# The first group's gates: transfers of combined weights and of split pieces issued by ScalarE instead of SyncE

## The reference, cut to what matters

```python
def mixer_a(h, w_in, ln_g, ln_b, w_s, b_s, w_out):
    u, v, z = jnp.split(h @ w_in, 3, axis=-1)
    u = jax.nn.gelu(u)
    v = layer_norm(jax.nn.gelu(v), ln_g, ln_b)
    ...
    mixed = jnp.einsum("gts,bnsgc->bntgc", ws, vc) + b_s.T[:, :, None]
    y = u * mixed.reshape(B, S, A_WIDTH) * jax.nn.silu(z)
    return y @ w_out
```

## Time and profile before

| what | value |
|---|---|
| median of three runs | 2218.93 us (2217.34 to 2219.06) |
| the profiled execution | 2219.44 us, its span 2217.7 us |
| PE | 2150.9 us busy, 97% |
| DVE, ACT, POOL | 1440.5 (65%), 1095.3 (49%), 1195.1 us (54%) |
| granted clock of PE, mean | 0.996 |
| SP's queue | 585.71 MB, 73.5% of the transfer engines' time |
| ACT's queue | 5.30 MB, 0.7% |

### The profile page before, as it was taken

The page is one execution under the profiler, slowest core; times in us unless marked ns, Lnnn a source line. Parts: engine busy times, 40 slices in busy tenths (PEclk is TensorE's granted clock), DMA queues, the critical chain, the costliest instruction groups (busy, mean ns, idle before and its releaser), DMA issues.

```text
span 2217.7 us, 29383 instructions
## 1 busy us (share of the span) xinstructions
PE 2150.9 (97%) x10410; PEld 1801.0 (81%) x10410; DVE 1440.5 (65%) x1761; ACT 1095.3 (49%) x2050; POOL 1195.1 (54%) x913
## 2 busy tenths in 40 slices
PE   5999999999999999999999999999999999999998
PEld 4887778788888878888777888887888888888887
DVE  6956548757486864554974673767767657656854
ACT  4334446634545744445653445534545646545653
POOL 3456675845553865544594645441535555454542
PEclk9999999999999999999999999999999999999999
DMA  9888889785558785557877556899686697887654
GB/s 347 307 306 308 312 315 356 231 308 174 196 198 324 285 315 191 200 179 269 314 259 283 181 181 218 323 348 365 244 297 225 253 359 266 280 309 288 206 205 171
DMA packets 244787, 592.89 MB, mean 267 GB/s; under 512 B 20929, under 2 KB 96801, under 8 KB 244257
## 3 DMA queue, kind: packets, MB, share of 16 engines
q1 hardware_dynamic: 241680, 585.71, 73.5%
q10 hardware_dynamic: 2960, 5.30, 0.7%
HBM read 461.96 MB, written 119.54 MB: 262 GB/s over the span
## 4 chain that ended last, share of the span: by engine, by line
PE 75%; DMA 6%; POOL 6%; DVE 5%; ACT 3%; DVEq 2%; POOLq 1%; issue 1%; SPq 1%; ACTq 0%
PE ps L2361 22%; PE ps L2363 22%; PE ps L2362 22%; DMA w_raw<-in_a_w_in 3%; POOL w_lo L1130 3%; PE ps L2566 2%; PE ps L2615 1%; PE ps L2616 1%; POOL cbl L1149 1%; PE ps L2641 1%; DVE acc L1812 1%; ACT w_hi L1364 1%; DMA w_lo<-a_weights_combined 1%; PE ps L2650 1%; DVE yb L2093 1%
## 5 line engine op out<-in xcount | busy, mean ns | idle before, releaser
L1130 POOL TENSOR_TENSOR w_lo<-w_raw,w_hi 128x1024 fp32r<-128x1024 f32 x244 | 650.0, 2682 | 569.6 <-ACT w_hi L1364 569.4
L1364 ACT ACTIVATE w_hi<-w_raw 128x1024 fp32r<-128x1024 f32 x260 | 272.0, 1057 | 418.3 <-DMA w_raw<-in_a_w_in 372.7
L2361 PE MATMUL ps<-h,w_hi 128*128 128x512 f32 x1024 | 403.3, 394 | 9.7 <-POOL w_lo L1130 8.3
L2363 PE MATMUL ps<-h,w_lo 128*128 128x512 f32 x1024 | 398.9, 390 | 0.0
L2362 PE MATMUL ps<-h,w_hi 128*128 128x512 f32 x1024 | 398.7, 389 | 0.0
L2361 PEld LDWEIGHTS ps<-h,w_hi 128*128 128x128 f32 x1024 | 192.2, 188 | 55.3 <-POOL w_lo L1130 14.3
L2363 PEld LDWEIGHTS ps<-h,w_lo 128*128 128x128 f32 x1024 | 192.2, 188 | 40.7
L2362 PEld LDWEIGHTS ps<-h,w_hi 128*128 128x128 f32 x1024 | 192.4, 188 | 38.9 <-issue 0.2
L2361 PE MATMUL ps<-r,w_hi 128*128 128x512 f32 x480 | 191.6, 399 | 1.9 <-issue 1.9
L2363 PE MATMUL ps<-r,w_lo 128*128 128x512 f32 x480 | 187.7, 391 | 0.0
L2362 PE MATMUL ps<-r,w_hi 128*128 128x512 f32 x480 | 187.3, 390 | 0.0
(11 more groups left out here) (277 smaller groups left out, 4902.6 us busy)
## 6 DMA issues: line engine op xcount, KB each, us to landing
w_raw<-in_a_w_in SPq DMA_DIRECT2D x256, 256.0 KB, 3.6
w_hi<-b_weights_split SPq DMA_DIRECT2D x104, 512.0 KB, 4.7
w_lo<-b_weights_split SPq DMA_DIRECT2D x104, 512.0 KB, 6.3
w_raw<-in_a_w_in SPq DMA_DIRECT2D x52, 512.0 KB, 4.7
w_raw<-in_a_w_out SPq DMA_DIRECT2D x48, 512.0 KB, 5.4
w_hi<-v_weights_combined SPq DMA_DIRECT2D x48, 512.0 KB, 3.9
w_lo<-v_weights_combined SPq DMA_DIRECT2D x48, 512.0 KB, 5.2
w_hi<-a_weights_combined SPq DMA_DIRECT2D x32, 512.0 KB, 6.6
```

Source lines behind the costliest of these rows:

```text
L1130: g.tensor_tensor(wlo[p][:, rows_], raw[p][:, rows_], whi[p][:, rows_].bitcast(F32), ALU.subtract).then_inc(w_lo, 1)
L1364: s_.activation(whi[p][:, rows_], raw[p][:, rows_], ACT.Copy).then_inc(w_hi, 1)
L2361: t_.matmul(dst_, stat[0], mov[0], start=start, stop=False)
L2363: return t_.matmul(dst_, stat[1], mov[0], start=False, stop=stop)
```

## The change

`load_split`, `keep_split`, `load_comb` and `keep_comb` move out of SP's block and get the issuing engine as an argument; their bodies stay as they are. In group 0 SP keeps only the combinations of stages up to 4 for loading (`q <= FIRST_BY_ACT + 1`) and those of stages below 3 for storing (`q - 2 < FIRST_BY_ACT`), and no split pieces. ACT takes the others: the loads of stage 4 + `g` ahead of `hi` of the next first unit (steps 1 to 7), the stores of stage 3 + `g` behind it, ahead of the gelus (steps 0 to 7). In groups 1 to 3 SP goes on as before.

```diff
+FIRST_BY_ACT = 3
...
+        def keep_comb(eng, c):
+            _, _, whose, n, m = COMBS[c]
+            eng.wait_ge(comb_lo, c + 1)
...
-            def keep_comb(c):
-                _, _, whose, n, m = COMBS[c]
-                sp.wait_ge(comb_lo, c + 1)
...
                 s = split_at(i, q - 2)
-                if s is not None:
-                    keep_split(s)
-                for c in combs_at(i, q - 2):
-                    keep_comb(c)
+                if s is not None and i >= 1:
+                    keep_split(sp, s)
+                if q - 2 < FIRST_BY_ACT:
+                    for c in combs_at(i, q - 2):
+                        keep_comb(sp, c)
                 if 1 <= q < GROUPS + 4:
                     unit(first + 2 * q + 1)
...
-                for c in combs_at(i, q):
-                    load_comb(c)
+                if q <= FIRST_BY_ACT + 1:
+                    for c in combs_at(i, q):
+                        load_comb(sp, c)
                 s = split_at(i, q)
-                if s is not None:
-                    if i == 0:
-                        sp.wait_ge(ada_used, 6 * KT)
-                    load_split(s)
+                if s is not None and i >= 1:
+                    load_split(sp, s)
...
                     if g == 0:
                         comb(i, 3)
                         split(i, 3)
+                    if i == 0 and g >= 1:
+                        for c in combs_at(0, 4 + g):
+                            load_comb(act, c)
+                        if split_at(0, 4 + g) is not None:
+                            act.wait_ge(ada_used, 6 * KT)
+                            load_split(act, split_at(0, 4 + g))
                     hi(uz_unit(i, g + 1, 0))
+                    if i == 0:
+                        for c in combs_at(0, 3 + g):
+                            keep_comb(act, c)
+                        if split_at(0, 3 + g) is not None:
+                            keep_split(act, split_at(0, 3 + g))
                     if g == GROUPS - 1:
                         factor_round(0, 0)
                         factor_round(1, 0)
```

More of the change, by code:

```diff
@@ L774, in landed, with load_split @@
             return 16 * sum(transfers(w) for w in range(u + 1) if BUFFER[w] == BUFFER[u])
+        wa = a_w_in[0].rearrange("(k p) n -> p k n", p=P)
+        wo2 = a_w_out[0].rearrange("(k e p) n -> p k e n", e=2, p=P)
+        wkv = w_kv.rearrange("(k p) n -> p k n", p=P)
+        wb = b_w_in[0].rearrange("(k p) n -> p k n", p=P)
+        wbo = b_w_out[0].rearrange("(k p) n -> p k n", p=P)
+        def load_split(eng, s):
+            m, (kind, n, ku), hh = SPLIT_SLOT[s], SPLIT_UNITS[s // 2], s % 2
+            kt = 4 * ku + 2 * hh
+            if split_before(s):
+                eng.wait_ge(split_out[m], 32 * split_before(s))
+            if kind == "kv":
+                there, src = wsr[m][:].rearrange("p a (b n) -> p (a b) n", b=2), wkv[:, 4 * hh:4 * hh + 4, :]
+            elif kind == "b":
+                there, src = wsr[m][:], wbo[:, kt:kt + 2, 512 * n:512 * n + 512]
+            else:
+                there, src = wsr[m][:, :, 0:256], wb[:, kt:kt + 2, 256 * n:256 * n + 256]
+                eng.dma_start(wsr[m][:, :, 256:512], wb[:, kt:kt + 2, D + 256 * n:D + 256 * n + 256]) \
+                    .then_inc(split_in[m], 16)
+            eng.dma_start(there, src).then_inc(split_in[m], 16)
@@ new lines, in keep_split, with load_comb @@
+        def keep_split(eng, s):
+            eng.wait_ge(split_lo, s + 1)
+            m = SPLIT_SLOT[s]
+            eng.dma_start(wsd[s, 0], wsh[m][:].bitcast(F32)).then_inc(split_out[m], 16)
+            eng.dma_start(wsd[s, 1], wsl[m][:].bitcast(F32)).then_inc(split_out[m], 16)
+        def load_comb(eng, c):
+            _, _, whose, n, m = COMBS[c]
+            if comb_before(c):
+                eng.wait_ge(comb_out[m], comb_out_before(c))
+            elif m == 0:
+                eng.wait_ge(xt_full, 8)
+            elif m >= 2:
+                eng.wait_ge(ada_used, 6 * KT)
+            col = WIDTH + 1024 * (n // 4)
+            for half in range(2):
+                src = wo2[:, n, half, :] if whose == "a" else wa[:, 4 * half + n % 4, col:col + 1024]
+                eng.dma_start(cbr[m][:, 2 * half:2 * half + 2], src.rearrange("p (a n) -> p a n", a=2)) \
+                    .then_inc(comb_in[m], 16)
@@ new lines, in keep_comb @@
+        def keep_comb(eng, c):
+            _, _, whose, n, m = COMBS[c]
+            eng.wait_ge(comb_lo, c + 1)
+            to, some = (cad[:, n // 4] if whose == "a" else cbd[n // 4]), rounded_combs(c)
+            for part, w in ((0, cbh[m]), (1, cbl[m])):
+                eng.dma_start(to[some, n % 4 // 2, part, :, n % 2].rearrange("t p n -> p t n"),
+                             w[:, some].bitcast(F32)).then_inc(comb_out[m], 16)
+            if whose == "a":
+                eng.dma_start(to[1:4:2, n % 4 // 2, 0, :, n % 2].rearrange("t p n -> p t n"), cbr[m][:, 1:4:2]) \
+                    .then_inc(comb_out[m], 16)
@@ L776, in _ @@
         @block.sync
         def _(sp):
[L778 to L782, removed]
             def a_half(u, hh):
@@ L988, in _ @@
                         if n == 11:
-                            load_split(split_at(i, 3))
+                            load_split(sp, split_at(i, 3))
                         if n == 9:
```

## The result

The changed kernel takes **2231.95 us** in the median of four runs (2230.75 to 2236.80); the kernel before took 2218.86 us beside it (2217.34 to 2219.06). The ratio is 1.0066, with a 95% interval of 1.0054 to 1.0078: slower by 13.1 us, inside the range and at the time of the second rival (2232), not at the forecast (2220). The profiled execution took 2233.09 us, its span is 2231.3 against 2217.7.

A forecast was written before the change was run, and what follows sets the result against it. PE is busy 2150.9 of 2217.7 us; its gate gaps offer at most 8.3. Step 2 at 185.5, five steps of 25.9, then 23.8 and 0.5 end at 339.3 against 338.7; with `yb` +1: 2220, range 2211 to 2235.

The forecast's parts named there:

- rival 2: On ACT between first unit's rounding and gelu: its wait replaces SP's, 28.4 us a step, +13, 2232; chance 0.27 including rival 4.
- The bound: PE's idle time before matmuls in the first group's gates, waiting for POOL's low parts: 8.3 us, 0.37%, at most to gain.
- Loads on ACT, cost 0: Four 512 KB loads behind `v_norm`, 1.9 us of issuing covered by running work, and early enough for DVE's forming: cost 0.
- Two 1 MB stores, 2.0 us: ACT's issuing of two stores between `cbl` and gelu in a step: 2.0 us taken, bounds 0.9 to 4.5.
- Split-piece stores, 0.5 us: Two small stores of split pieces on ACT in step 7, adding 0.5 us to the end of the stage.
- the prediction's own sign of being wrong: Prediction wrong if stores block ACT for over 3 us, or DVE's forming no longer meets POOL at all.
- `yb` behind the last stores, 0 to 1 us: Step 7's rounding of `yb` on ACT, behind the last stores, adds another 0 to 1 us.
- The ring, 21.7 us: Loop from last tanh through DVE, ACT and POOL's `cbl`, stores, gelu to tanh; tanh to `cbl` end 21.7, step 25.9 us.
- Landing in 5 to 7 us: Second unit's weights, issued by SP when PE ends a step, land after 5 to 7 us, against 7.5 before.
- Rival 3: Second units' weights land no sooner, so their seven gaps (6.4 us) partly stay: -1 to +5, about 2221; chance 0.10.
- Signs named beforehand: Trace signs: SP's `cbl` waits moved to ACT, second-unit gaps gone, gelu releasing first units, landing times, nothing outside the first group moving.
- Rival 4: ACT's late loads hold up DVE's forming, ending in rival 2's time; its 0.04 is within that rival's 0.27.

The follow-up runs named there:

- The loads alone: Changed kernel with SP storing as before and ACT only loading: 2228.57 us, ratio 1.0044 to the kernel before.
- second profile: For the changed kernel: the same kernel profiled once more, nothing changed; 2230.65 us in a single run, 2216.41 for the kernel before beside it.
- The wait alone: Kernel before, all transfers still issued by SP, plus ACT's wait for POOL's `cbl` ahead of the gelus: 2225.34 us, ratio 1.0035.
- the small stores: Changed kernel with stores of combined weights cut to 64 KB from the third combination on, results wrong: single runs 2229.58 and 2232.38 us.
- the stores behind the tanhs: Changed kernel with ACT's stores of a step moved from ahead of its gelus and tanhs to behind them: 2221.88 us, ratio 1.0017.
- the stores alone: Changed kernel with SP loading again, ACT still waiting for POOL and storing ahead of the gates: 2229.49 us in a single run.

## Why the prediction came out as it did

- **The bound was right, the hope wrong.** SP's waits for POOL did end, and SP issued on time. The 8.3 us at stake were not to be had in full by any version tried: the shortest stage was 3.5 us under the one before.
- **Loads on ACT, cost 0**: right on ACT's own time. At 179.78 an issue begins inside ACT's `v_norm`:

```profile
179.48 0.59 ACT L1559 ACTIVATE vs<-vy,v_nm,v_rs 128x256 f32<-128x256 f32 x1
179.78 0.45 ACTq L816 DMA_DIRECT2D cbr<-in_a_w_in  x1
```

  Wrong as a whole: the term left out what late loads in a second queue take from the first. The loads alone cost 9.8 us where SP still stores, and 3 to 5 where it doesn't (192.1 and 193.7 against 189.3 and 188.4).
- **Two 1 MB stores, 2.0 us** (bounds 0.9 to 4.5): 0.90 to 1.7 in the first profile, up to 2.86 in the second (0.39 + 2.47). The bounds held; in five of seven steps of the first profile it was about 1.0, so the term was rather too large.
- **Split-piece stores, 0.5 us**: they took 1.34 + 1.56 = 2.9 us in step 5 and 1.15 + 1.22 = 2.4 in step 7. In step 5 some 3.5 MB of combinations had been issued into the same queue just before, and gelu waited 6.62 us. The sum has the term once, for step 7, where it was 1.9 us too small; for step 5 it has none. With the two stores before them ACT's issues stood ahead of its next ACTIVATE from 289.43 to 294.18 in step 5 and from 345.72 to 349.21 in step 7. So the prediction's own sign of being wrong, stores that block ACT for over 3 us, was there twice.
- **`yb` behind the last stores, 0 to 1 us**: PE waited 2.65 us for it and the gelu behind it, at 351.84.
- **The ring, 21.7 us**: here the sum broke. From the start of the last tanh to the end of `cbl` the first profile has 23.8, 22.6, 22.4, 25.1, 25.8 and 21.7 in steps 2 to 7, the second 24.1, 23.8, 22.1, 26.4, 24.1 and 20.9; the mean is 23.6 in both. In the kernel before the seven steps have 24.0, 23.1, 24.2, 23.6, 24.8, 25.3 and 24.0, mean 24.1. So the ring became 0.5 us shorter, not 2.3. The reason given for a shorter ring, weights that land before the tanh, so that DVE's forming doesn't meet POOL's subtraction, failed: the weights came later, and the forming took 63.0 us in the stage against 52.7. "Both were measured with weights that were late" was no argument for the other kernel, whose weights were late as well. Rival 2 costs more than 0.2% from a ring of 22.5 us, and 23.6 is above it.
- **Landing in 5 to 7 us**: 8.1 to 11.6 on the chain. The value under the 7.47 us of the earlier trace rows leaned on the 3.4 us of an empty queue. What was in SP's queue ahead of the weights went into ACT's, where it is served ahead of them or beside them. The prediction had worked out that some 1.3 MB would be left in ACT's queue at that moment, and 1.25 MB it was; but it priced them as ACT's issuing alone, not as the 3.5 us for which the weights got nothing. The rule of the Trainium skill quoted in the prediction ("DMA: Bandwidth & Descriptors", "Issuing engines are not separate DMA queues"), that a second issuer saves issuing time only, agrees with this trace in the main: 4.3 MB moved in 11 us by two queues against 3.9 by one. Rival 3 was built on it and took the landing to stay; the rows show that it grows. What rival 3 lacked is the division: nothing for 3.5 us, then by pieces, with 30% of the bytes for the queue with pieces of 1 KB.
- **The clock** had no term at all. Two stretches at half clock behind gaps of 1.90 and 3.06 us cost 1.7 us each in the first profile. A sum of waits alone comes out short once single gaps reach that size. The second profile has two such stretches as well (from 187.41 and 214.72, behind gaps of 2.47 and 2.21).
- **The size of rival 2** (+13) came out to within 1 us, but half of it by chance: its ring of 28.4 us a step is not found; the steps after the first are 28.9, 26.7, 25.3, 25.6, 28.9 and 28.6, mean 27.3. The wait alone is worth 6 us (7.9 by the medians), not 13. The rest comes with what ACT's queue moves, which it didn't hold.
- **Signs named beforehand**: SP's waits gone, yes; a gelu as releaser before first units, yes; second-unit gaps gone, no, they are longer; landing of 7.5 us or more, as rival 3 had it; nothing moved before the stage or behind it but 1.2 and 0.2 us. Rival 4's DVE waits: none.

What stays open: why a store of 1 MB takes ACT 0.53 us to issue at one time and 2.47 at another. A full queue fits, and with the small stores the long issues were gone, but no run varied what the queue holds by itself. Open too is how the part beyond the wait divides between the other queue, the loads' later time and ACT's longer issues. And with the stores behind the tanhs, where no wait stands ahead of the gates, the stage ended 2.5 us under the kernel before: SP's lateness, which the change does remove, may be that difference; no run separates it.

## What to carry to other kernels

Before moving transfers into a second engine's queue, write down what was behind them in the first one, and look at what will then run beside it: a critical transfer that stood behind part of it now stands behind or beside all of it, and with small pieces it gets the small share. A wait put on the engine that frees the accumulators closes a loop through all engines; measure the loop on the kernel as it is, and don't subtract waiting from it unless the change is sure to remove that waiting. If an engine must both store late results and read banks, let it read the banks first: here that order is worth 15 us of the stage and about 9 of the total (13.1 less 4.5).

## What the runs showed of the hardware that was not expected

- Two queues that both move share the transfer engines about by the piece, not by the byte: 1533 packets of 3.02 MB beside 1313 of 1.28 MB in 11 us, with about the same sum (4.3 MB) as one queue alone.
- Before they share, the queue with earlier work can have the engines alone: weights issued from 183.46 moved nothing until 187, while the other queue moved 1.25 MB, and stores issued from 283.22 nothing until 287, while it moved 1.22 MB. Two stores of 1 MB behind these landed after 10.1 and 13.6 us instead of 4.3 and 7.7.
- PE's clock stood at half for 3.41 us just after single gaps, or around their ends. Over all profiles such gaps measure from 1.88 us (the stores behind the tanhs, stretch from 371.13) to 4.30 us (the stores alone, second profile). Around the ends of gaps of 3.47, 4.51 and 5.42 us it stood at half for 6.83. But gaps of 1.88 and 3.27 us at 229.19 and 294.92 in the changed kernel had no such stretch, so the length of a gap alone does not tell.
- A DVE operation of 0.69 us takes 2.7 to 2.9 us when POOL subtracts at the same time, so that earlier weights can make a later sum.
